# GpSimd makes low parts of the first rows and of one weight tile, the rotary angles go behind them, and VectorE and ScalarE share the modulation

## The reference, cut to what matters

```python
mod = jnp.einsum('bd,de->be', jax.nn.silu(c), w_ada) + b_ada
shift, scale, gate = jnp.split(mod, 3, axis=-1)
h = rms_norm(x, pre_g) * (1 + scale[:, None, :]) + shift[:, None, :]
proj = jnp.einsum('bsd,de->bse', h, w_in)
...
qa = apply_partial_rope(heads(qa, N_HEADS_A), cos, sin)   # cos, sin of positions * inv_freq
```

## Time and profile before

| | |
|---|---|
| median of 3 runs | 1567.25 us (1566.03 to 1567.61) |
| the profiled execution's own time | 1567.49 us |
| its span in the profile | 1565.7 us |
| TensorE busy in the span | 1547.2 us (99%) |
| VectorE busy | 1172.5 us (75%) |
| ScalarE busy | 768.7 us (49%) |
| GpSimd busy | 89.8 us (6%) |
| mean granted TensorE clock | 0.998 |

### The profile page before, as it was taken

The page is one execution under the profiler, slowest core; times in us unless marked ns, Lnnn a source line. Parts: engine busy times, 40 slices in busy tenths (PEclk is TensorE's granted clock), DMA queues, the critical chain, the costliest instruction groups (busy, mean ns, idle before and its releaser), DMA issues.

```text
span 1565.7 us, 20528 instructions
## 1 busy us (share of the span) xinstructions
PE 1547.2 (99%) x7858; PEld 1286.9 (82%) x7858; DVE 1172.5 (75%) x1917; ACT 768.7 (49%) x1228; POOL 89.8 (6%) x130
## 2 busy tenths in 40 slices
PE   8999999999999999999999999999999999999998
PEld 5788778888888888887777888888888888888887
DVE  7889899859986665487756898878887667666654
ACT  5767766532222222264556565445555563455542
POOL 2000000300000000030010100010000100010000
PEclk9999999999999999999999999999999999999999
DMA  9987677337666665252133787857787685566550
GB/s 376 368 310 262 244 261 250 114 121 251 233 215 234 223 227 176 94 184 81 55 105 104 291 311 292 335 194 289 265 286 273 218 305 193 174 218 193 188 195 28
DMA packets 94708, 341.97 MB, mean 218 GB/s; under 512 B 11074, under 2 KB 11714, under 8 KB 94355
## 3 DMA queue, kind: packets, MB, share of 16 engines
q1 hardware_dynamic: 90706, 327.58, 59.0%
q0 software_dynamic: 3904, 13.08, 2.4%
HBM read 339.54 MB, written 1.09 MB: 218 GB/s over the span
## 4 chain that ended last, share of the span: by engine, by line
PE 94%; DVE 2%; ACT 1%; DMA 1%; issue 1%; POOL 0%; SPq 0%; POOLq 0%; DVEq 0%; ACTq 0%
PE bank L294 90%; PE bank L297 4%; DMA sb_w<-in_w 1%; ACT sb_hi L300 1%; DVE sb_w L314 0%; ACT sb_arena L300 0%; DMA sb_X<-in_x 0%; DVE sb_tmw L314 0%; ACT sb_sg L300 0%; ACT sb_XN L300 0%; DVE sb_tm L303 0%; DVE sb_w8r L303 0%; DVE sb_w2r L303 0%; DVE sb_X L311 0%; DVE sb_sg L308 0%
## 5 line engine op out<-in xcount | busy, mean ns | idle before, releaser
L300 ACT ACTIVATE sb_hi<-sb_w 128x1024 fp32r<-128x1024 f32 x428 | 431.3, 1051 | 287.7 <-DMA sb_w<-in_w 246.3
L294 PE MATMUL bank<-sb_hT,sb_hi 128*128 128x512 f32 (+1 forms) x1984 | 516.1, 377 | 0.0
L294 PEld LDWEIGHTS bank<-sb_hT,sb_hi 128*128 128x128 f32 x1984 | 360.1, 189 | 64.9 <-issue 0.9
L294 PE MATMUL bank<-sb_hi,sb_hT 128*128 128x512 f32 x1024 | 331.0, 398 | 3.9 <-ACT sb_arena L300 2.2
L294 PEld LDWEIGHTS bank<-sb_hi,sb_hT 128*128 128x128 f32 x1024 | 192.8, 189 | 49.6 <-issue 4.3
L314 DVE CUSTOM_DVE_ANT_0 sb_w<-sb_w,sb_cb 128x1024 f32<-128x1024 f32 x144 | 175.0, 1220 | 0.0
L303 DVE TENSOR_TENSOR sb_sg<-bank,sb_sg 128x512 f32<-128x512 f32 (+1 forms) x90 | 58.7, 660 | 96.4 <-ACT sb_sg L300 76.5
L300 ACT ACTIVATE sb_sg<-bank 128x512 f32<-128x512 f32 (+2 forms) x100 | 55.9, 573 | 110.5 <-PE bank L294 110.1
L300 ACT ACTIVATE sb_arena<-bank 128x512 f32<-128x512 f32 (+1 forms) x108 | 57.1, 558 | 53.3 <-PE bank L294 33.0
L303 DVE TENSOR_TENSOR sb_tm<-bank,sb_rows 128x512 f32<-128x512 f32 (+1 forms) x41 | 28.0, 684 | 65.3 <-PE bank L294 62.5
L300 ACT ACTIVATE sb_XN<-sb_X 128x512 f32<-128x512 f32 x33 | 20.7, 629 | 106.6 <-DVE sb_X L303 100.3
(11 more groups left out here) (491 smaller groups left out, 3028.9 us busy)
## 6 DMA issues: line engine op xcount, KB each, us to landing
sb_w<-in_w SPq DMA_DIRECT2D x428, 512.0 KB, 4.6
sb_w<-in_mw SPq DMA_DIRECT2D x192, 512.0 KB, 5.0
sb_rows<-gate_rows POOLq DMA_DIRECT2D x9, 512.0 KB, 5.5
sb_rows<-in_na_rpb POOLq DMA_DIRECT2D x16, 96.0 KB, 2.8
sb_X<-in_x SPq DMA_DIRECT2D x1, 1024.0 KB, 4.9
sb_cb<-in_cvec POOLq DMA_DIRECT2D x2, 512.0 KB, 9.4
sb_XC<-in_ctx POOLq DMA_DIRECT2D x1, 1024.0 KB, 13.4
sb_arena<-in_sg_ln_g POOLq DMA_DIRECT2D x1, 1024.0 KB, 5.9
```

What stands on the lines that cost most here:

```text
L294: return self.e.matmul(out, a, b, start=start, stop=stop)
L300: return self.e.activation(out, a, f, **kw)
```

## The change

Four things are done, all in the first layer's opening (stage "a0").

- The low parts of pair 0 (two operations of 128 x 256), of weight tile 3, and of pairs 1, 2 and 3 (128 x 512 each) go from VectorE to GpSimd.
- On GpSimd the angles stand behind the low part of pair 1 and ahead of that of pair 2. The transfer of `blk`, which waits until TensorE is done with tile 9, stands between the low parts of pairs 2 and 3.
- Scale and shift of pair 1 are done one half by VectorE and one by ScalarE; those of pairs 2 and 3 by VectorE alone.
- ScalarE's sine and cosine go from behind tile 3's high part to behind tile 11's.

```diff
@@ dve_tick
+                if n == POOL_TILE:
+                    continue
...
+        POOL_TILE = 3
+
+        def pool_first_low_tile(e):
+            n = POOL_TILE
+            s = SLOT["w", n]
+            e.wait_ge(*done(HI, n))
+            e.tt(ring_r[s][:, :, :], ring[s][:, :, :], HI_[HB[n]][:, :, :].bitcast(F32), ALU.subtract).then_inc(
+                PO.sem, PO.put("low", n))
...
+        def first_turned_by(c2, h):
+            return DE if c2 > 1 or h == 0 else AE
+
+        def dve_first_turned(e, c2):
+            e.wait_ge(*done(AE, "raw", c2))
+            for h in range(2):
+                if first_turned_by(c2, h) is DE:
+                    ch, t = c2 * 2 + h, turned_rows("a0", 0, c2, h)
+                    e.wait_ge(*modulated("a0sh", ch))
+                    e.wait_ge(*modulated("a0sc", ch))
+                    e.ts(t, t, mods[:, TG["a0sc"], ch:ch + 1], mods[:, TG["a0sh"], ch:ch + 1], ALU.mult, ALU.add).then_inc(
+                        DE.sem, DE.put("t", "a0", 0, c2, h))
...
+        def act_first_high(e, c2):
+            t, h, _ = turned_rows("a0", 0, c2)
+            for x in range(2):
+                e.wait_ge(*done(first_turned_by(c2, x), "t", "a0", 0, c2, x))
+            e.act(h, t, ACT.Copy).then_inc(AE.sem, AE.put("hh", "a0", 0, c2))
...
-            e.wait_ge(DE, DE.n)
-            e.tt(l, t, h.bitcast(F32), ALU.subtract).then_inc(DE.sem, DE.put("chunk", "l"))
+
+        def pool_first_chunk(e):
+            t, h, l = turned_rows("a0", 0, 0)
+            e.wait_ge(*done(DE, "chunk", "h"))
+            e.tt(l[:, 0, :], t[:, 0, :], h[:, 0, :].bitcast(F32), ALU.subtract).then_inc(PO.sem, PO.put("chunk", "l"))
+            e.wait_ge(*done(AE, "hh", "a0", 0, 0))
+            e.tt(l[:, 1, :], t[:, 1, :], h[:, 1, :].bitcast(F32), ALU.subtract).then_inc(
+                PO.sem, PO.put("hl", "a0", 0, 0))
...
@@ h_ready
-                return done(AE, "hh", s, p, c2) if part == "h" else done(DE, "hl", s, p, c2)
+                return done(AE, "hh", s, p, c2) if part == "h" else done(PO, "hl", s, p, c2)
@@ act_block1
-                act_rope_tables(e)
                 for c2 in range(1, 4):
                     act_tick(e, 4 * c2, 4 * c2)
-                    act_turned(e, s, 0, c2)
-                    act_high(e, s, 0, c2, [])
+                    act_first_turned(e, c2)
+                    act_first_high(e, c2)
                     act_tick(e, 4 * c2, 4 * c2 + 3)
+                    if c2 == 2:
+                        act_rope_tables(e)
@@ dve_block1
                 dve_tick(e, 0, 1, vectors=False)
-                dve_low(e, s, 0, 0)
...
                 for c2 in range(1, 4):
+                    dve_first_turned(e, c2)
                     dve_tick(e, 4 * c2, 4 * c2, vectors=False)
                     if c2 < 3:
                         dve_vector(e, 4 * c2 + 4)
-                    dve_low(e, s, 0, c2)
@@ pool_start
             pool_rstd(e, "a0")
+            pool_first_chunk(e)
+            pool_first_low_tile(e)
+            pool_low(e, "a0", 0, 1)
             pool_rope_tables(e)
+            pool_low(e, "a0", 0, 2)
             e.wait_ge(*done(USED, 9))
             e.dma(blk.rearrange("p a b -> p (a b)"), I["blk"][:, :]).then_inc(LD["blk"].sem, LD["blk"].put(0, by=16))
+            pool_low(e, "a0", 0, 3)
```

More of the change, by code:

```diff
@@ L554, in dve_tick, with first_low @@
                 dve_vectors(e, t)
+        POOL_TILE = 3
[5 more added lines that the diff above has]
+                PO.sem, PO.put("low", n))
+        def first_low(t):
+            return done(PO, "low", t) if t == POOL_TILE else done(LO, t)
         def dve_vectors(e, t):
@@ L734, in turned_rows, with act_first_turned @@
             return SG[c2][:, at:at + 2 * w].rearrange("p (a b) -> p a b", a=2), hTh[c], hTl[c]
+        def first_turned_by(c2, h):
[9 more added lines that the diff above has]
+                        DE.sem, DE.put("t", "a0", 0, c2, h))
+        def act_first_turned(e, c2):
+            for h in range(2):
+                if first_turned_by(c2, h) is AE:
+                    ch, t = c2 * 2 + h, turned_rows("a0", 0, c2, h)
+                    e.wait_ge(*done(AE, "raw", c2))
+                    e.wait_ge(*modulated("a0sh", ch))
+                    e.wait_ge(*modulated("a0sc", ch))
+                    e.act(t, t, ACT.Identity, scale=mods[:, TG["a0sc"], ch:ch + 1],
+                          bias=mods[:, TG["a0sh"], ch:ch + 1]).then_inc(AE.sem, AE.put("t", "a0", 0, c2, h))
+        def act_first_high(e, c2):
[3 more added lines that the diff above has]
+            e.act(h, t, ACT.Copy).then_inc(AE.sem, AE.put("hh", "a0", 0, c2))
         def act_turned(e, s, p, c2):
@@ L739, in act_turned @@
             e.wait_ge(*done(TRP, "norm", s, p, c2))
-            if s == "a0" and c2:
-                e.wait_ge(*done(AE, "raw", c2))
             for h in range(2):
@@ L745, in act_turned @@
                 e.wait_ge(*modulated(n + "sc", ch))
-                src = turned_rows(s, p, c2, h) if s == "a0" and c2 else BANK["norm", s, p, c2].ap[:, h * w:(h + 1) * w]
+                src = BANK["norm", s, p, c2].ap[:, h * w:(h + 1) * w]
                 e.act(turned_rows(s, p, c2, h), src, ACT.Identity,
@@ L773, in dve_first_chunk @@
         def dve_first_chunk(e):
-            t, h, l = (z[:, 0, :] for z in turned_rows("a0", 0, 0))
+            t, h, _ = (z[:, 0, :] for z in turned_rows("a0", 0, 0))
             e.wait_ge(*done(TRP, "norm", "a0", 0, 0))
@@ L788, in act_high @@
                 e.wait_ge(*f)
-            e.wait_ge(*done(AE if s == "a0" else DE, "t", s, p, c2, 1))
+            e.wait_ge(*done(DE, "t", s, p, c2, 1))
             e.act(h, t, ACT.Copy).then_inc(AE.sem, AE.put("hh", s, p, c2))
@@ L800, in dve_low @@
             t, h, l = turned_rows(s, p, c2)
-            if s == "a0" and c2 == 0:
-                t, h, l = t[:, 1, :], h[:, 1, :], l[:, 1, :]
-            e.wait_ge(*done(AE if s == "a0" else DE, "hh", s, p, c2))
+            e.wait_ge(*done(DE, "hh", s, p, c2))
             e.tt(l, t, h.bitcast(F32), ALU.subtract).then_inc(DE.sem, DE.put("hl", s, p, c2))
@@ L833, in h_ready @@
             if s == "a0" and kc == 0:
-                return done(DE, "chunk", part)
+                return done(DE, "chunk", "h") if part == "h" else done(PO, "chunk", "l")
             if s == "a0":
-                return done(AE, "hh", s, p, c2) if part == "h" else done(DE, "hl", s, p, c2)
+                return done(AE, "hh", s, p, c2) if part == "h" else done(PO, "hl", s, p, c2)
             if c2 % 2 == 0:
@@ L846, in all_split @@
             return [f for s in stages for p in parts_of(s)
-                    for f in (done(DE, "hl", s, p, 2), done(DE if s == "a0" else PO, "hl", s, p, 3))]
+                    for f in (done(PO if s == "a0" else DE, "hl", s, p, 2), done(PO, "hl", s, p, 3))]
         def rows_turned(s):
@@ L1009, in pe_first_tiles @@
                     e.mm(banks[x].ap[:, :], al(k, x), h[:, k, :], False, False)
-                e.wait_ge(*done(LO, u))
+                e.wait_ge(*first_low(u))
                 for x in range(2):
```

## The result

The changed kernel takes **1573.69 us** (median of 5 runs, 1572.74 to 1575.33) against 1567.25 before (5 runs, 1566.03 to 1567.61): ratio 1.0045, 95% interval [1.0034, 1.0056], 6.4 us slower. The forecast was 1573.9. The profiled execution took 1573.69 us as well, with a span of 1571.9 against 1565.7.

A forecast was written before the change was run, and what follows sets the result against it. TensorE, busy 1547.2 of 1565.7 us, was taken to bound the kernel, so its waits are lost. 4.8 (late low part of pair 2) + 1.6 (clock) = +6.4 on 1567.49 gave 1573.9 us; range 1566.3 to 1577.5.

The forecast's parts named there:

- Modulation of pair 1: VectorE's opening: held by GpSimd's subtractions, less work given away, it ends at 26.7 instead of 25.72, +1.0 us.
- Scale and shift: Pair 1, shared by VectorE and ScalarE: 1.35 us, high part at 28.1 instead of 27.57, tile 4 0.4 us late.
- Low part of pair 1: On GpSimd, done at about 30.0, no TensorE wait at tile 4; tile 8's "a" products wanted at 41.6.
- The angles: 14 GpSimd operations from 30.0, mostly one VectorE operation (1.14 us) each: 13.6 us, ending at 43.6.
- Low part of pair 2 and the wait: GpSimd finishes it at 45.5, so TensorE's tile 8 "a" products begin then instead of 40.70: +4.8 us.
- The clock: Behind TensorE's 3.9 us standstill at tile 8, half clock costs 7 matmuls of 0.23: +1.6 us, bounds 0 to 3.2.
- Pair 3, sine and cosine: Later in the opening, both cost nothing, covered by TensorE's own delay; without that, pair 3 costs up to 1 us.
- a shift of the opening should reach the end whole: After 60 us no TensorE wait for a weight transfer was found, so the opening's delay should pass undiminished to the end.
- the likeliest case: Low part of pair 2 late on GpSimd in the opening: 1570.5 to 1577.5 us, chance 0.60.
- the angles pass quickly: Rival: GpSimd's angles take 9.9 us as before, TensorE waits 0.2 us at tile 8: +1.1, 1568.6 us; chance 0.14.
- Not slower: Rival: GpSimd works beside VectorE unhindered at pair 1's modulation, 0.8 us kept: 1566.7 us; chance 0.15.
- GpSimd starves: Rival: pair 1's low part takes 8.34 us on GpSimd, all behind it 6.4 us later: +12.8, 1580.3 us; chance 0.08.

The follow-up runs named there:

- the two kernels with 12 and 16 operations: Changed kernel with two of its 14 angle operations left out, 1570.57 us (ratio 1.0022), or two more added, 1576.51 us (ratio 1.006).
- the six subtractions: Kernel before the change plus six unused GpSimd subtractions of 128 x 512 behind its angles: 1573.09 us, ratio 1.0039.
- the fills: Kernel before the change plus twelve unused GpSimd fills of 128 x 1024 behind its angles: 1566.0 us, ratio 0.9998.
- the angles first: Changed kernel with angles, sine and cosine at their old places and low parts of tile 3 and pair 0 back on VectorE: 1567.65 us, ratio 1.0005.

## Why the prediction came out right

The mechanism was right and the sum was within 0.2 us, but both terms of it were too small (5.44 for 4.8 and 2.54 for 1.6), and a third thing, which the prediction denied, made up for them. That the number fits so closely is luck.

1. *Modulation of pair 1, +1.0.* It ended at 27.09 instead of 26.7, so +1.37. The hold by tile 3 was 2.20 (1.96 taken, 2.6 the upper bound), that by pair 0's first half 0.50 (0.55 taken). What VectorE saved by giving away pair 0's first low part was 0.17, not 0.35: it reached tile 0's low part at 12.02 and then waited 0.17 for its high part. With these, 0.50 + 2.20 - 1.14 - 0.17 = 1.39.
2. *Scale and shift.* From there to the high part 1.42 us (27.09 to 28.51) for 1.35; VectorE's half took 0.41 for 0.3, but ScalarE's 0.60 is what is waited for. Tile 4 was 0.93 late, not 0.4 (the recorded 28.1 against 27.57 would already give 0.5).
3. *Low part of pair 1.* Done at 29.90 for 30.0, since it met the boundary at 28.66 at once; no wait at tile 4's "a" products. Tile 5 waited 0.29, since VectorE began its low part at 30.91, 2.36 later than before, and not some 1.4 (1.0 + 0.98 - 0.61): to the 0.37 of step 1 comes the half of scale and shift, 0.5 us with its hand-over, which no term of VectorE's lateness held. So TensorE came to tile 8's "a" products 1.41 late and not 0.9: it wanted them at 42.1 (40.70 + 1.41), not 41.6. The wait of 3.86 is counted from the end of the last matmul, 42.28.
4. *The angles.* 14.0 us for 13.6, with three short ones as counted, beside the short operations on the modulation and the two scale-and-shifts of pair 2 (37.90 to 39.15): the price of one VectorE operation each is what the two kernels with 12 and 16 operations show (1.12).
5. and 6. *Low part of pair 2 and the wait.* Done at 46.09 for 45.5, and the products 5.44 late for 4.8. That the wait itself came out at 3.86 for 3.9 is an accident: both its ends were 0.5 to 0.6 off.
7. *The clock, +1.6.* It was 2.54 (7.98 - 5.44). The row that the price was taken from had a stretch at half the clock 3.5 us long; this one was some 6.8 us long (44.5 to 51.3), of which TensorE stood still for 1.6. The bound of 3.2 held it.
8. *Pair 3, sine and cosine, nothing.* Right here: no wait of TensorE behind 46.14 in the opening. That TensorE's own delay was the cover is not borne out: with pair 2 back on VectorE the delay was gone and pair 3 still cost no wait. What it needs is that GpSimd is free in time: with the angles right ahead of it the wait was 3.95 us.

The opening thus cost 8.0 us and not 6.4. **The step that failed** is the one sentence that a shift of the opening should reach the end whole. It lost 0.5 us by 70 us, nearly all of it at one place, where the idle time of 0.30 at 55.67 in the trace before was filled. It lost another 1.3 near 720 us (7.3 to 6.0): 1.5 behind the wait, less 0.2 by which the wait itself is longer. There the kernel before ran some 3.4 us at half the clock in its profiled execution, and the changed one did not. That is chance: which of its executions have this stretch changes for one and the same kernel (see the end). So the sum fitted partly because errors cancelled.

The range was not added up rightly either. With its own bounds (angles 9.9 to 16.8 us, clock 0 to 3.2) the likeliest case runs from 1568.6, which is the first rival's time, to 1573.9 + 3.2 + 1.6 = 1578.7, and not from 1570.5 to 1577.5. The measured time lies inside both.

Of the rivals, "the angles pass quickly" needed them in under 10 us: they took 14.0. "Not slower" needed a hold under 1 us: it was 2.20, and the six subtractions show it again. "GpSimd starves" did not happen here; every long operation of GpSimd got in at the first boundary between two of VectorE's. The Trainium skill's rule on order of issue ("SBUF — State Buffer", "Who interferes with whom") thus described the opening better than the row at 283.70 did. Yet that row came back in the changed kernel, in GpSimd's timeline and VectorE's:

```profile
291.13 8.35 POOL L303 TENSOR_TENSOR sb_hT<-sb_sg,sb_hT 128x512 fp32r<-128x512 f32 x1 [72.36 <-ACT sb_hT L300]
...
291.09 1.22 DVE L303 TENSOR_TENSOR sb_w4r<-sb_w,sb_hi 128x1024 fp32r<-128x1024 f32 x1
...
296.77 1.22 DVE L303 TENSOR_TENSOR sb_w6r<-sb_w,sb_hi 128x1024 fp32r<-128x1024 f32 x1
297.90 0.42 DVE L321 CAST sb_hT<-sb_sg 128x512 fp32r<-128x512 f32 x1
298.36 1.67 DVE L303 TENSOR_TENSOR sb_hT<-sb_sg,sb_hT 128x512 fp32r<-128x512 f32 x1
```

There six subtractions of VectorE stand in a row, from 291.09 to 297.99, and GpSimd's operation passed the five boundaries between them without a turn. It ends at 299.48; less the 1.30 us that the form takes alone, it began near 298.2, an estimate, beside the CAST, which has one input. So it did work beside the last of the "seven" operations of the prediction. The rule on order of issue does not hold there, and what decides it stays open. The prediction's guess, that in the opening VectorE's stream has changes of operation between, does not explain it. With the angles behind pair 2's low part, a waiting angle operation got its turn at a boundary between two subtractions of the same form: it came at 53.68, beside the first, and had ended by 54.79, just behind the start of the second (GpSimd's timeline and VectorE's):

```profile
53.68 1.11 POOL L307 TENSOR_SCALAR sb_ang<-sb_ang 128x16 f32<-128x16 f32 x1
...
53.40 1.27 DVE L303 TENSOR_TENSOR sb_w12r<-sb_w,sb_hi 128x1024 fp32r<-128x1024 f32 x1
54.60 1.21 DVE L303 TENSOR_TENSOR sb_w14r<-sb_w,sb_hi 128x1024 fp32r<-128x1024 f32 x1
```

In the changed kernel pair 3's low part got in at such a boundary too (53.62 us), but right behind GpSimd's own issue of a transfer (52.80 to 53.60), so it is not a clean case of an operation that waited.

None of the kernels tried was faster than the one before. The gain that sharing brings by itself, 0.4 us at tile 4 and 0.5 at 39 us, is given back by 244 us.

## What to carry to other kernels

Price a small operation on GpSimd by what VectorE is doing beside it, and not by its own size: beside operations with two inputs in SBUF each of them lasted for one of VectorE's (1.12 us for 0.3), and a chain of 14 was a delay of 14 us for whatever stood behind it in the queue. Put the chain where nothing behind it is wanted yet, and count what comes behind it: moving one low part ahead of the chain only made the next one late. A wait of several us ahead of TensorE costs more than itself, and a price for that taken from one row should be given a range: here the wait of 3.86 us brought another 2.5, where the row that was taken for it had cost 1.6.

## What was unexpected

- **How long the clock stays low differs.** The stretches at half clock were some 3.4 us behind waits of 2.15 us (before, near 715) and 1.95 (pair 2 back on VectorE), some 6.8 us around the waits of 3.86, 3.86, 5.27 and 3.95, and some 10 us around that of 6.62 ahead of tile 4 in the kernel with six subtractions. They can begin during the wait, so part of them costs nothing.
- **The same wait, with and without it.** Behind 1.96 us at tile 4 the changed kernel kept 1.00, as the one with two operations fewer did (1.97 us); those with pair 2 back on VectorE (1.95), with two operations more and with the angles behind pair 2 (1.97 both) did not. Behind 2.37 us at 722 the changed kernel kept it, before did not behind 2.15. The profiled executions of before and of the sharing alone have the stretch near 715 (1567.49 and 1567.83 us); those with the fills and with the angles first lack it (1565.99 and 1566.92). The times of the kernel before fall in two groups to match: of 27 runs on one chip, ten took 1565.4 to 1566.2 and seventeen 1567.2 to 1567.7. So a difference below some 1.6 us between two kernels here can be a difference in how often each has the stretch, and the expected 0.2 to 0.6 us of the sharing alone could not have been told. No run here settles what decides it. The Trainium skill, in "TensorE: Matmul & The Clock Gate", Part 1, says that the clock's watch runs free of the kernel and that the same kernel therefore meets the slower clock differently from run to run; these rows agree with that, and none of them proves it.
- **Holding is one-sided.** The 11 long angle operations cost VectorE next to nothing (its operations beside them stay at 1.21 to 1.27 us) and took 1.0 to 1.2 each; one of 128 x 512 cost it 1.1, and one of 128 x 1024 cost it 2.2.
